# Moving projection pieces, their copies and two value tiles in the attention of a two-layer diffusion trunk

## The reference

```python
qkv = hl @ w_qkv                                   # latent tokens, 16 heads of 64
kv_c = hc @ w_qkv[:, D:]                           # context tokens: keys and values
for each row r of the 64-wide grid:
    s_win = q_r . k_window * scale + bias          # 8 rows x 16 columns of neighbours
    s_ctx = q_r . k_ctx * scale                    # 256 context keys
    p = softmax(concat(s_win, s_ctx))
    o = p_win . v_window + p_ctx . v_ctx
yl = o @ w_o
```

## Time and profile before

| | us |
|---|---|
| median of 3 runs | 2953.51 (2953.23 to 2953.83) |
| the profiled execution | 2952.8 |
| its span, first to last instruction | 2950.9 |
| TensorE busy in the span | 2835.5 (96%) |
| VectorE, ScalarE, GpSimd busy | 2008.8, 996.8, 1134.6 |
| granted TensorE clock, mean | 0.989 of full speed |

### The profile page before, as it was taken

One profiled execution on the slowest core, in us unless ns is written; L12 is line 12 of the kernel. 1 busy time (PEld: TensorE's weight loads), 2 busy tenths in 40 slices (PEclk: granted clock), 3 DMA queues, 4 the chain that ended last, 5 costly groups with the idle time before them and its releaser, 6 DMA issues.

```text
span 2950.9 us, 43755 instructions
## 1 busy us (share of the span) xinstructions
PE 2835.5 (96%) x14962; PEld 2361.0 (80%) x14962; DVE 2008.8 (68%) x3114; ACT 996.8 (34%) x1710; POOL 1134.6 (38%) x794
## 2 busy tenths in 40 slices
PE   6999999999999999999998999998898999999998
PEld 3888888677788888899987888888776878888886
DVE  4766775778777777746662666666556877777777
ACT  4211111413222222345422666666513232222223
POOL 1212111127555565300021444545321475565652
PEclk9999999999999999999998999999999999999999
DMA  6312214021111111486676555556650111111111
GB/s 241 116 61 85 75 57 97 22 86 43 57 50 50 57 50 51 136 285 210 191 206 183 142 156 143 149 155 171 194 198 22 43 50 50 50 50 57 50 57 65
DMA packets 195000, 310.60 MB, mean 105 GB/s; under 512 B 71248, under 2 KB 129616, under 8 KB 194896
## 3 DMA queue, kind: packets, MB, share of 16 engines
q1 hardware_dynamic: 194896, 309.22, 33.6%
HBM read 259.87 MB, written 53.22 MB: 106 GB/s over the span
## 4 chain that ended last, share of the span: by engine, by line
PE 84%; DVE 5%; ACT 3%; issue 3%; DMA 3%; POOL 1%; SPq 1%; DVEq 0%; ACTq 0%; POOLq 0%
PE psum L1174 21%; PE psum L1026 20%; PE psum L985 17%; PE psum L1359 5%; PE psum L1224 4%; PE psum L1312 3%; PE psum L1235 2%; PE psum L1415 2%; PE psum L1384 2%; PE psum L1012 2%; PE psum L1398 2%; DMA o_dram<-o_st_lo 1%; ACT pt_hi L1905 1%; DVE residual L2119 1%; PE psum L920 1%
## 5 line engine op out<-in xcount | busy, mean ns | idle before, releaser
L2119 DVE SCALAR_TENSOR_TENSOR residual<-psum,modulation,residual 128x512 f32<-128x512 f32 x896 | 639.8, 729 | 378.8 <-PE psum L1026 374.9
L2673 POOL TENSOR_TENSOR w_lo<-raw,w_hi 128x1024 fp32r<-128x1024 f32 x118 | 296.2, 2517 | 970.3 <-ACT w_hi L1539 967.5
L1026 PE MATMUL psum<-prod_hi,w_hi 128*128 128x512 f32 x896 | 350.1, 391 | 9.7 <-DVE residual L2119 4.9
L1026 PE MATMUL psum<-prod_hi,w_lo 128*128 128x512 f32 x896 | 343.6, 383 | 0.0
L1026 PE MATMUL psum<-prod_lo,w_hi 128*128 128x512 f32 x896 | 343.3, 383 | 0.0
L2706 POOL TENSOR_TENSOR w_lo<-raw,w_hi 128x512 fp32r<-128x512 f32 x175 | 259.2, 1481 | 209.7 <-ACT w_hi L1700 209.7
L1539 ACT ACTIVATE w_hi<-raw 128x1024 fp32r<-128x1024 f32 x186 | 194.5, 1057 | 428.0 <-PE psum L985 189.5
L1174 PE MATMUL psum<-act_hi,w_hi 128*128 128x512 f32 x700 | 273.6, 391 | 6.2 <-POOL w_lo L2706 6.1
L1174 PE MATMUL psum<-act_lo,w_hi 128*128 128x512 f32 x700 | 272.7, 390 | 0.0
L1174 PE MATMUL psum<-act_hi,w_lo 128*128 128x512 f32 x700 | 272.6, 389 | 0.0
L2556 DVE TENSOR_TENSOR pt_lo<-psum,pt_hi 128x512 fp32r<-128x512 f32 (+1 forms) x224 | 145.7, 652 | 138.4 <-ACT pt_hi L1905 137.8
(11 more groups left out here) (266 smaller groups left out, 6576.6 us busy)
## 6 DMA issues: line engine op xcount, KB each, us to landing
raw<-ffn_panels SPq DMA_DIRECT2D x198, 512.0 KB, 3.3
raw<-conv_panels SPq DMA_DIRECT2D x32, 512.0 KB, 5.9
rest_in<-mod_rest SPq DMA_DIRECT2D x40, 384.0 KB, 4.4
more_row<-mod_panels SPq DMA_DIRECT2D x48, 256.0 KB, 2.8
k_hi<-k_dram SPq DMA_DIRECT2D x32, 320.0 KB, 5.8
k_lo<-k_dram SPq DMA_DIRECT2D x32, 320.0 KB, 7.4
v_st<-v_dram SPq DMA_DIRECT2D x32, 320.0 KB, 7.1
mod_in<-mod_rest SPq DMA_DIRECT2D x24, 384.0 KB, 5.8
```

Of the source, the lines that this page charges most:

```text
L1026: mm = pe.matmul(psum[:, 6 + r % 2 if bank is None else bank, 0:tn], w[:, s, ob, :], h[:, t0:t0 + tn], start=(n == 0), stop=(n == 2))
L2119: dve.scalar_tensor_tensor(out=residual[:, ob, t0:t0 + tn], in0=psum[:, 6 + r % 2 if bank is None else bank, 0:tn], scalar=modulation[:, g ...
L2673: pool.tensor_tensor(panel(w_lo, s), raw[:, s], panel(w_hi, s), ALU.subtract).then_inc(lo_done[s], 1)
```

## The change

The list of values is cut two tiles short: the tiles 20 and 21 are computed between the projection tiles of the start, in banks 6 and 7, with an own buffer `late_v_hi`. The last of the seven early projection tiles, (1, 1), is taken to the attention's bank 7, its matmuls stand half before and half behind the scores of unit 1, and its copies stand in unit 0 of the attention. The pieces of the projection are shared out over the groups in other counts, and each tile's copies stand one group sooner (the one of tile (1, 4) keeps its group, and its matmuls end one group later). All counts of matmuls, copies and DMAs stay as they were.

```diff
-        FIRST_BANKS = (2, 3, 4, 5, 2, 4, 5)
+        FIRST_BANKS = (2, 3, 4, 5, 2, 4, QK_BANK)
-        QK_CHUNKS = {**chunks(1, 2, 0, (5, 5, 5, 5, 4)), **chunks(1, 3, 6, (6, 6, 6, 6)), **chunks(1, 4, 11, (8, 8, 8)),
-                     **chunks(2, 0, 15, (5, 5, 5, 5, 4)), **chunks(2, 1, 21, (5, 5, 5, 5, 4))}
-        QK_DRAINED = {6: (1, 2), 11: (1, 3), 15: (1, 4), 21: (2, 0), 27: (2, 1)}
+        QK_CHUNKS = {**chunks(1, 2, 0, (9, 5, 3, 4, 3)), **chunks(1, 3, 6, (5, 7, 6, 6)), **chunks(1, 4, 11, (8, 4, 4, 8)),
+                     **chunks(2, 0, 16, (4, 7, 7, 6)), **chunks(2, 1, 21, (6, 6, 4, 4, 4))}
+        QK_DRAINED = {5: (1, 2), 10: (1, 3), 15: (1, 4), 20: (2, 0), 26: (2, 1)}
...
+        V_LATE = len(V_ORDER) - 2
+        LATE_V_BANKS = (6, 7)
...
             load_qk_panel(1, 1)
             sp.wait_ge(bias_in, 32 * HEADS)
-            sp.wait_ge(v_ready, len(V_ORDER))
+            sp.wait_ge(qk_ready, 1)
             load_bias(0, 0)
...
             load_heads(0, 0)
             sp.wait_ge(rest_summed, MORE_GROUPS + V_LAST)
+            store_v(V_LATE)
             load_v(0, 0)
             store_qk(1, 0)
+            store_v(V_LATE + 1)
+            for n in range(V_STAGES):
+                sp.wait_ge(v_out[n], 32 * len(V_ORDER) // V_STAGES)
             load_heads(0, 1)
...
             for n, bank in enumerate(FIRST_BANKS):
                 if bank == V_REST_BANK:
                     pe.wait_ge(rest_ready, 2 * MORE_GROUPS + V_LAST)
+                if n == NQK + 1:
+                    break
+                if n == NQK:
+                    v_tile(V_LATE)
                 if bank in FIRST_BANKS[:n]:
                     pe.wait_ge(qk_lo_done, n - FIRST_BANKS[:n][::-1].index(bank))
                 qk_matmuls(n // NQK, n % NQK, bank, 0, QK_MATMULS)
+            v_tile(V_LATE + 1)
...
             pe.wait_ge(qk_lo_done, NQK)
-            for u in range(2):
-                for ab in range(2):
-                    scores(0, u, ab)
-            pe.wait_ge(qk_lo_done, len(FIRST_BANKS))
+            for ab in range(2):
+                scores(0, 0, ab)
             pe.wait_ge(v_lo_done, len(V_ORDER) + 4)
+            qk_matmuls(1, 1, QK_BANK, 0, QK_MATMULS // 2)
+            for ab in range(2):
+                scores(0, 1, ab)
+            qk_matmuls(1, 1, QK_BANK, QK_MATMULS // 2, QK_MATMULS)
+            pe.wait_ge(qk_lo_done, NQK + 1)
...
                     pt_high(i, u, 0)
+                    if first and u == 0:
+                        qk_high(1, 1)
                     drain(group0[u])
```

More of the change, by code:

```diff
@@ L478, in trunk @@
         WO_COLUMNS = {p + 2: V_LAST + g for g, p in enumerate(wo_ends)}
-        assert len(REST_SUMS) == V_GROUPS and max(REST_COLUMNS) < len(V_ORDER)
+        assert len(REST_SUMS) == V_GROUPS and max(REST_COLUMNS) < V_LATE
         assert len(WO_SUMS) == REST_GROUPS - V_LAST and max(WO_COLUMNS) <= PAIRS
@@ L688, in store_v @@
                 sp.wait_ge(v_lo_done, n + 5)
-                for part, stage in enumerate((stage_v_hi, stage_v_lo)):
+                for part, stage in enumerate(v_stage(n)):
                     sp.dma_start(v_dram[heads, :, t, part].rearrange("h p d -> p h d"),
@@ L693, in _ @@
             V_LOADS = {2: (0, 1), 3: (2, 3)}
-            for n in range(len(V_ORDER)):
+            for n in range(V_LATE):
                 store_v(n)
@@ L1308, in v_products @@
                 if kb == 0:
-                    at_least(pe, v_lo_done, n - len(V_BANKS) + 5)
+                    at_least(pe, v_lo_done, n - (len(V_BANKS) if n < V_LATE else len(LATE_V_BANKS)) + 5)
                 for part, (h, w) in enumerate(((act_hi, whi), (act_lo, whi), (act_hi, wlo))):
                     panels = w[:, first:end, kb, :] if half == 0 else w[:, first:end, kb * P:(kb + 1) * P]
-                    mm = pe.matmul(psum[:, V_BANKS[n % len(V_BANKS)], 0:(end - first) * P], h[:, kb, t * P:(t + 1) * P],
+                    mm = pe.matmul(psum[:, v_bank(n), 0:(end - first) * P], h[:, kb, t * P:(t + 1) * P],
                                    panels, start=(kb == 0 and part == 0),
@@ L1328, in _ @@
             ctx_pieces(HIDDEN - 1)
-            for n in range(1, len(V_ORDER)):
+            for n in range(1, V_LATE):
                 if n == V_BANKS.index(CTX_BANKS[2]):
@@ L1845, in v_high @@
                 cols = (V_ORDER[n][2] - V_ORDER[n][1]) * P
-                act.activation(stage_v_hi[:, n % V_STAGES, 0:cols].bitcast(F32R),
-                               psum[:, V_BANKS[n % len(V_BANKS)], 0:cols], ACT.Copy).then_inc(v_hi_done, 1)
-            for n in range(len(V_ORDER)):
+                act.activation(v_stage(n)[0][:, n % V_STAGES, 0:cols].bitcast(F32R),
+                               psum[:, v_bank(n), 0:cols], ACT.Copy).then_inc(v_hi_done, 1)
+            for n in range(V_LATE):
                 v_high(n)
@@ L1881, in qk_high @@
                                scale=(SCALE, 1.0)[s]).then_inc(qk_hi_done, 1)
-            for n, bank in enumerate(FIRST_BANKS):
-                qk_high(n // NQK, n % NQK, bank)
+            for n in range(NQK):
+                qk_high(0, n, FIRST_BANKS[n])
                 if n == K_FIRST - 1:
@@ L2474, in v_low @@
                 dve.tensor_tensor(stage_v_lo[:, n % V_STAGES, 0:cols].bitcast(F32R),
-                                  psum[:, V_BANKS[n % len(V_BANKS)], 0:cols],
-                                  stage_v_hi[:, n % V_STAGES, 0:cols], ALU.subtract).then_inc(v_lo_done, 1)
-            for n in range(len(V_ORDER)):
+                                  psum[:, v_bank(n), 0:cols],
+                                  v_stage(n)[0][:, n % V_STAGES, 0:cols], ALU.subtract).then_inc(v_lo_done, 1)
+            for n in range(V_LATE):
                 v_low(n)
@@ L2509, in _ @@
             dve.wait_ge(residual_out, 16 * KB)
-            for n, bank in enumerate(FIRST_BANKS):
-                qk_low(n // NQK, n % NQK, bank)
-                if n == NQK - 1:
-                    dve.memset(zeros[:], 0.0).then_inc(attn_consts, 1)
-                    dve.memset(probs[:, :, KEYS_IN:], 0.0).then_inc(attn_consts, 1)
-                    dve.memset(pt_hi[:, 5:7, :].bitcast(F32), 0.0).then_inc(attn_consts, 1)
-                    dve.memset(pt_lo[:, 5:7, :].bitcast(F32), 0.0).then_inc(attn_consts, 1)
+            for n in range(NQK):
+                qk_low(0, n, FIRST_BANKS[n])
+            dve.memset(zeros[:], 0.0).then_inc(attn_consts, 1)
+            v_low(V_LATE)
+            qk_low(1, 0, FIRST_BANKS[NQK])
+            v_low(V_LATE + 1)
+            dve.memset(probs[:, :, KEYS_IN:], 0.0).then_inc(attn_consts, 1)
+            dve.memset(pt_hi[:, 5:7, :].bitcast(F32), 0.0).then_inc(attn_consts, 1)
+            dve.memset(pt_lo[:, 5:7, :].bitcast(F32), 0.0).then_inc(attn_consts, 1)
             dve.wait_ge(attn_consts, 5)
@@ L2581, in attention @@
                     pt_low(i, u, 0)
+                    if first and u == 0:
+                        qk_low(1, 1)
                     drain(group0[u])
```

15 lines of the change are left out of this document (12 added, 3 removed).

## The result

The changed kernel takes 2964.49 us (median of 7 runs, 2959.94 to 2967.32), the one before 2953.83 beside it (7 runs, 2952.04 to 2959.23). The ratio is 1.0031, 95% interval 1.0022 to 1.0040: slower by 0.31%. The median had been predicted as 2958.8, inside a range of 2938 to 2967. The profiled execution took 2960.96 us, 8.2 more than the one before; for it 2958.1 had been predicted.

The account below looks back on a forecast made before the run. TensorE, busy 2835.5 us, was taken as the bound, so only its idle or slow stretches could pay. 2952.8 - 13.1 (start) + 18.4 (pairs) = 2958.1 profiled, median 2958.8; 8-in-10 range 2938 to 2967, own range 2953 to 2964.

Parts of the forecast that it names:

- worse on both sides: Rival, slower: start gains only 9.5 us, pairs cost 3.8 us each as group 0's wait stays; 2968.5 us, chance 0.15.
- The predicted marks: Signs: `stage_hi` idle about 1.5 us five times a pair, full clock, `values` waits 1.9 (group 11), 1.7 (25), none (0).
- The start: Attention's start: projection begins 10.98 us sooner, waits for heads hidden, first `values` at 1611.05; gain 13.1 us, bounds 9.5 to 14.9.
- A pair: Steady pair: copies one group sooner make ScalarE wait for TensorE; five group terms sum to +2.79 us, bounds -3.9 to +4.
- group 5: Group 6's bank wait of 0.69 us goes, transposes of group 8 wait 0.45 for VectorE's work: -0.24 us a pair.
- group 10: ScalarE's copy waits for group 9's pieces, so `o_half` and `values` of group 11 come later: +1.48 us a pair.
- group 14: Tile (1, 4) ends here; the copy, `o_half` and `head_sum` wait for its eight pieces, 1.1 instead of 0.69: +0.41 us.
- group 20: Copy waits for group 19's pieces; `values` of group 21 0.89 later, less 0.23 for a sixth piece moved: +0.66 us.
- group 26, with group 0: Copy waits for group 25's pieces, a new 1.7 us wait; group 0's wait goes, 0.93 of work moved: +0.48 us.
- Pairs 6 and 7: Last pairs: pair 6 has only tiles (1, 2) to (1, 4), +1.65 us; pair 7 has none of the tiles.
- All waits covered: Rival, faster: copies' waits cost nothing, some 16 us saved in pairs and 13.1 at the start; 2925 us, chance 0.13.
- First in, first out: Rule that ScalarE and VectorE take instructions strictly in order; cited case: ScalarE's copy at 1611.02, 13.48 us late, exponentials behind it.

Follow-up runs that it names:

- F: The kernel before with only the copies of tile (1, 2) moved from group 6 to group 5: 2952.72 us, ratio 0.9995, pair 65.40 us.
- C: The kernel before with only the copies of tile (1, 3) moved from group 11 to group 10: 2964.21 us, ratio 1.0030, pair 67.19 us.
- E: The kernel before with only the copies of tile (2, 0) moved from group 21 to group 20: 2959.20 us, ratio 1.0016, pair 66.79 us.
- D: The kernel before with only the copies of tile (2, 1) moved from group 27 to group 26: 2965.05 us, ratio 1.0036, pair 67.23 us.
- J: New start with the tables of the kernel before, but tile (1, 2) in pieces 9, 5, 3, 4, 3: 2935.94 us, ratio 0.9933, pair 64.79 us.
- L: New start, old tables, but (1, 2) in pieces 11, 5, 1, 4, 3 and (1, 3) in 8, 8, 8 from group 7: 2930.47 us, pair 63.79.
- G: The kernel before with tile (1, 3) in pieces 8, 8, 8 from group 6 and its copies in group 10: 2960.28 us, ratio 1.0025.
- H: The kernel before with tile (1, 3) in pieces 8, 8, 8 from group 6, its copies left in group 11: 2960.32 us, ratio 1.0032.
- I: The changed kernel with its copies in groups 6, 11, 16, 21 and 27: 2941.12 us, ratio 0.9961 to the kernel before, pair 65.46 us.

## Why the prediction was right, and where it was too small

**The direction and the mechanism** held: faster at the start, slower in the pairs by copies that wait. The size did not: the median was forecast 5.3 us above the one before and came out 10.7 above it, half a us outside the forecast's own range (2953 to 2964) and nearer to the rival "worse on both sides" (2968.5) than to the forecast. Of the 5.7 us between 2964.49 and 2958.8, 2.9 are the profiled execution's (2960.96 against 2958.1), and 2.8 that the median lay 3.5 above it and not 0.7. The predicted marks are there: `stage_hi` idle by TensorE for 1.47, 1.30, 1.47 and 1.65 us in the rows above (and once more in group 5), `values` waiting 1.8 us in group 25 (1.7 forecast) and 0.12 in group 0, clock at 1.00. In group 11 `values` wait 1.4 us where 1.9 was forecast; another 0.4 stands before the transposes of that group, and the delay as a whole is the forecast 1.5.

**The start.** Predicted 13.1 us, of which 0.93 is moved work; measured 1623.21 - 1611.41 + 0.93 = 12.7. TensorE's idle before the first scores was 0.1 us. The late stores did not disturb the heads.

**A pair.** Predicted +2.79, measured +3.56. Term by term, from the end of the pieces to the `values` they delay:

| term | predicted | in the changed kernel | alone |
|---|---|---|---|
| group 5 | -0.24 | -0.14 | -0.30 (F) |
| group 10 | +1.48 | +1.50 (1777.18 - 1771.39 = 5.79, was 4.29) | +1.49 (C) |
| group 14 | +0.41 | +0.54 | |
| group 20 | +0.66 | +0.89 (6.07, was 4.95, less 0.23 moved) | +1.09 (E) |
| group 26, with group 0 | +0.48 | +0.72 (8.64, was 6.99, less 0.93 moved) | +1.53 (D), -0.94 (J) |

The other 0.05 is spread. The terms of groups 20 and 26 were the mis-sized ones, by steps that the prediction took from elsewhere (the waited copy to start 0.19 us behind the pieces, and 0.48 from it to the next instruction): the copy came 0.28 or 0.29 behind them in all three groups (1771.67 - 1771.39, 1796.68 - 1796.39, 1811.62 - 1811.34), and in group 20 and 26 the next instruction followed after 0.62, not 0.48. The two slips are the 0.23 of group 20's miss. In group 26 what `values` waited for last was VectorE's low copy and `o_sum` behind it, not `o_half`: they came 2.18 us behind the pieces where 2.05 was forecast, and from there to group 0 it took 6.46 where the sum has 6.35. All of it comes six times.

The copies measured alone (C, D, E, F) come to 3.81 a pair, and less the 0.94 of J to 2.87. With the 0.54 of group 14, whose change (the last eight pieces of tile (1, 4) in group 14, its copy still in 15) no run tests alone, that is 3.41 of the 3.56.

**Pairs 6 and 7.** Predicted +1.65 and 0, and pair 6 gives back the 0.93 us of work that the start has taken: +0.7. Measured by the distance between the first `values`, pair 6 is 68.33 against 67.90, and from there to the output projection it is 43.95 against 44.74 (2139.83 - 2095.88; 2129.96 - 2085.22): -0.4, which is 1.1 us better than the sum. Of it 0.79 lies in pair 7, where both kernels run the same order, and is not the change's: E and F, which have before's code there too, take 43.95 and 43.96 with a granted clock of 0.95 and 0.94. The windows of pair 7 in before and in the changed kernel, columns as in the earlier trace rows:

```profile
2085.22:2129.96 44.74, 38.18 (x271) 35.19 (x271) 33.15 (x94) 31.88 (x65) 18.75 (x22) 0.91 0.51 171
2095.88:2139.83 43.95, 37.43 (x271) 34.03 (x271) 33.15 (x94) 31.48 (x65) 18.73 (x22) 0.94 0.51 172
```

So before's profile happened to be 0.79 us slow there. The other 0.3, in pair 6, was not taken apart.

**The sum.** Up to the output projection: 2139.83 - 1.13 - 2129.96 = +8.7, predicted +5.3. Of the 3.4 between them, pairs 0 to 5 hold 4.2 (20.9 measured from first `values` to first `values`, 16.7 predicted), the start 0.4, and the last two pairs give 1.1 back. That the profiled execution came out as near as it did is in part luck. The final 8.2 holds two more things that profiles of one and the same code also show (the last section): 1.1 more ahead of the attention and 1.7 less behind it.

**The rivals.** "All waits covered" did not come, but what it says of the pieces is true where no copy waits: nine in group 0 hid all of theirs (J), and L's pair, 63.79, is 1.9 us under the one of before. "Worse on both sides" had the pair's size nearly right (3.8), but for a wait of group 0 that in the changed kernel went, and the start wrong (9.5).

**First in, first out.** The case that the prediction gave for this rule is not the longest blocked queue of the trace (ScalarE's panel split waits up to 19.6 us for a load, GpSimd longer still), and it is VectorE's rather than ScalarE's. VectorE's low copy waited 13.38 us for ScalarE's high copy, and VectorE's work on the scores, which TensorE had issued from 1607.26, stood behind it; the exponentials in turn waited for VectorE. The timeline of VectorE before:

```profile
1611.65 0.69 DVE L2505 SCALAR_TENSOR_TENSOR stage_lo<-psum,stage_hi 128x512 fp32r<-128x512 f32 x1 [13.38 <-ACT stage_hi L1880]
1612.26 0.68 DVE L2536 CUSTOM_DVE_ANT_0 neg_s<-psum,bias_full 128x512 f32<-128x512 f32 x1
```

For ScalarE it is C that bears the rule out (1.47 us).

## What to carry to other kernels

On an engine that takes its instructions in order, an instruction must not stand where its producer is still at work, unless what is behind it has time: read the chain from that place to the next thing another engine waits for. Work moved in front of a waiting beginning paid only where it lay beside that chain; moved ahead of the chain's start (G and H) it uncovered what it had hid. Test the halves of a combined change alone: here one was worth 14 us and the other cost 19.

## What the runs showed of the hardware

The issue of the value load `v_st` held SP for 5.21 us (1592.99, two DMAs) right behind a late value store, and for 5.0 to 5.7 us in the five other kernels with the new start; in the kernel before, the same issue took 1.07 us. Behind it stood only stores and the second head load, which is wanted later, so it cost nothing here. And the same code runs sooner or later from profile to profile: the first projection matmul stood up to 3.7 us apart in kernels that share the code ahead of it, the old start took 54.7 to 56.6 us, and the stretch from the output projection to the end 818.8 to 823.7. The runs of before beside E and H lie between 2949 and 2962. So a total of one profile decides nothing under several us. The length of a repeated pair serves better: among pairs 1 to 4 it agreed to 0.12 us or less in ten of the fourteen kernels (in H to 0.24, in F 0.27, in J 0.41 and in I 0.49), and kernels with the same tables have the same pair 2 within 0.03 (65.70 and 65.73, 69.26 and 69.24).
